# Three pairs of heads in flight in the sparse attention's loop, with the weights of the inner pairs normalised on GpSimd and both parts of the outputs made on VectorE

## The chip, the cores and the metric

One core of a Trainium2 chip runs the whole program. The metric is device time in microseconds (us), the median of three runs of one launch; lower is better.

## What is computed

Two blocks of a small transformer on 256 tokens of width 1024, in float32. The first block's first layer is a sparse attention: an indexer scores all keys for each query, the best 64 are kept, and the 16 heads (64 wide, two key and value heads) attend to those alone:

```python
topk = min(INDEX_TOPK, T // 4)
...
score = jnp.where(causal[None], score, -jnp.inf)
_, sel = lax.top_k(score, topk)
...
logits = jnp.where(valid[:, :, None, None, :], logits, -jnp.inf)
p = jax.nn.softmax(logits, axis=-1).astype(dt)
o = jnp.einsum('bqgrk,bqkgd->bqgrd', p, v_sel)
...
return out @ w_o
```

Behind it come a feed-forward layer, a gated linear recurrence with its own feed-forward layer, and then a second block (a gated linear attention beside a latent attention, and a feed-forward layer). They are not touched by the change.

## The kernel before

The program is written engine by engine, each with its own queue and explicit waits on semaphores; nothing reorders it. All weights come in tiles of 128x2048 through a ring of six staging buffers (`stage`). A product in float32 precision is made from two rounded parts of each operand: ScalarE rounds a tile to its upper part `wh` (`hi`, line 389), GpSimd subtracts it from the tile for the lower part `wl` (`lo`, line 393), and TensorE makes three products (lines 409 to 411). The activations have the two parts `xh` and `xl` in the same way. `low_ready` makes TensorE wait for the lower part of the tile that it is about to use; tile 8, the last of the output projection (`LAST_WO`), gets its lower part from VectorE (line 2598), all others from GpSimd.

The sparse attention's loop (`attend_pe`, `attend_act`, `attend_dve`) goes over eight pairs of heads. `sbias`, made from the selection, masks what a query doesn't attend to. For a pair i:

- TensorE makes the logits of both heads (`logits`, lines 808 and 810) in PSUM banks 0 and 1 or 2 and 3, by turns.
- VectorE scales and masks them and finds the negative of the largest of each row (`masked`, line 903) in a buffer `lg` in SBUF, of which there are three; the two query blocks have 128 and 256 keys, so each step has four instructions a pair, two of 128x128 and two of 128x256.
- ScalarE takes the exponentials with their sums (`exps`, line 874).
- VectorE takes the reciprocals of the sums (line 910) and scales the weights (`normalised`, line 916), a TENSOR_SCALAR in place in `lg`.
- TensorE transposes the weights (line 859) into banks 4 and 5, which all pairs share; ScalarE copies them to `pts` (line 883).
- TensorE multiplies them with the values (`value`, lines 820 to 824) into bank 6 or 7.
- ScalarE copies the result to `xh` (line 1021) and VectorE subtracts for `xl` (line 1136).

TensorE's queue holds logits 0 and 1, eleven fillers that keep it busy (`keep_warm`, line 687), and then for each i: logits i+2, transposes i, value i-1. ScalarE's holds exponentials 0, two copies of turned queries, exponentials 1, and then for each i: weight copy i, output copy i-1, exponentials i+2. VectorE's holds for each i: masking i+2, normalisation i+1, the lower part of output i-1. In the listings of the trace `arena` is the SBUF region in which `lg`, `pts`, the queries and the keys lie, and `ps` is PSUM.

GpSimd has no part in the loop: it makes the lower part of tile 6, waits for all eight normalisations, and then makes that of tile 7 (in the block at the end of `build`). Behind the loop TensorE makes the output projection with tiles 5 to 8 (`rows_t`), which waits for the last outputs' lower part, and ScalarE, which rounded the tiles up to 7 ahead of the loop, loads two rows of gains and goes on with tile 8.

Of the kernel before, what the change touches and what calls it, by code (L numbers as in the profile page):

```python
# [11 lines left out]
ALU = mybir.AluOpType  # L12
ACT = mybir.ActivationFunctionType
# [3 lines left out]
T = 256  # L17
D = 1024
P = 128
# [5 lines left out]
HEADS, HD, KVH = 16, 64, 2  # L25
# [150 lines left out]
def build(nc, A, out, marks):  # L176
    ctx = ExitStack()
    at = [SCRATCH + 128]
    with ctx:
# [89 lines left out]
        score = cut(12800, 3 * P)  # L269
        top8 = cut(13184, 2, 8)  # L270
        wi = cut(13200, 2, IH)
        lg = [cut(at, 2, 3 * P) for at in (13216, 13984, 12288)]
        pts = cut(14752, 2, 2, 3 * P)
        kit, kis = cut(16288, T), cut(16544, 2, P)
        relu0 = cut(14752, IH, P)
# [43 lines left out]
        def signals(names):  # L319
            return [Signal(sem(n)) for n in names.split()]  # L320
# [19 lines left out]
        lg_ps, nmx_ready, p_ready, pn_ready, pt_ps, pts_done, ot_ps, oh_done = signals(  # L340
            "lg_ps nmx_ready p_ready pn_ready pt_ps pts_done ot_ps oh_done")
        s_done, h_mul, h_ready = signals("s_done h_mul h_ready")


# [493 lines left out]
        def attend_pe(pe, pairs, logits, weighted, warm=0):  # L838
            def value(i):
                pe.wait_ge(pts_done.sem, pts_done.due(pe))  # L840
                if i >= 2:

                    pe.wait_ge(x_ready.sem, x_ready.due(pe))
                weighted(i, pts[:, i % 2, :, :]).then_inc(ot_ps.sem, ot_ps.up())

            for i in range(2):
                logits(i).then_inc(lg_ps.sem, lg_ps.up())
            keep_warm(4, warm)
            for i in range(pairs):
                if i + 2 < pairs:  # L850
                    pe.wait_ge(nmx_ready.sem, nmx_ready.due(pe))
                    logits(i + 2).then_inc(lg_ps.sem, lg_ps.up())
                pe.wait_ge(pn_ready.sem, pn_ready.due(pe))
                if i >= 1:

                    pe.wait_ge(pts_done.sem, pts_done.seen(pe) + 1)
                for e in range(2):
                    for c in range(3):
                        last = nc.tensor.transpose(ps[:, 4 + e, c * P:(c + 1) * P],
                                                   lg[i % 3][:, e, c * P:(c + 1) * P], ident[:])  # L860
# [6 lines left out]
        def attend_act(act, pairs, between, outputs):  # L867
            def exps(i):
                act.wait_ge(nmx_ready.sem, nmx_ready.due(act))
                for e in range(2):  # L870
                    for t, (c0, c1) in enumerate(((0, P), (P, 3 * P))):
                        at = 8 + 8 * (i % 2) + 2 * e + t
                        x = lg[i % 3][:, e, c0:c1]
                        ins = nc.scalar.activation(x, x, ACT.Exp, bias=small[:, at + 4:at + 5], scale=-1.0,  # L874
                                                   accum_out=small[:, 16 + at:17 + at])
                ins.then_inc(p_ready.sem, p_ready.up())

            exps(0)
            between()
            exps(1)  # L880
            for i in range(pairs):
                act.wait_ge(pt_ps.sem, pt_ps.due(act))
                nc.scalar.activation(pts[:, i % 2, :, :], ps[:, 4:6, 0:3 * P], ACT.Copy  # L883
                ).then_inc(pts_done.sem, pts_done.up())
                if i >= 1:
                    act.wait_ge(ot_ps.sem, ot_ps.due(act))
                    outputs(i - 1)
                if i + 2 < pairs:
                    exps(i + 2)
            act.wait_ge(ot_ps.sem, ot_ps.due(act))  # L890
            outputs(pairs - 1)

        def attend_dve(dve, pairs, scale, bias, outputs):
            def masked(i):
                dve.wait_ge(lg_ps.sem, lg_ps.due(dve))
                x = lg[i % 3]
                if i >= 3:

                    dve.wait_ge(pt_ps.sem, pt_ps.seen(dve) + i - 2)
                for e in range(2):  # L900
                    for t, (c0, c1) in enumerate(((0, P), (P, 3 * P))):
                        at = 12 + 8 * (i % 2) + 2 * e + t
                        ins = V.tensor_tensor_reduce(x[:, e, c0:c1], ps[:, 2 * (i % 2) + e, c0:c1], bias[:, c0:c1],
                                                     -scale, 3.0e38, ALU.add, ALU.min, small[:, at:at + 1])
                ins.then_inc(nmx_ready.sem, nmx_ready.up())

            def normalised(i):
                dve.wait_ge(p_ready.sem, p_ready.due(dve))
                at = 24 + 8 * (i % 2)
                V.reciprocal(small[:, at + 4:at + 8], small[:, at:at + 4]).then_inc(dve_step.sem, dve_step.up())  # L910
                dve.wait_ge(dve_step.sem, dve_step.now())
                for e in range(2):
                    for t, (c0, c1) in enumerate(((0, P), (P, 3 * P))):
                        x = lg[i % 3][:, e, c0:c1]
                        w = at + 4 + 2 * e + t
                        ins = V.tensor_scalar(x, x, small[:, w:w + 1], None, ALU.mult)
                ins.then_inc(pn_ready.sem, pn_ready.up())

            masked(0)
            masked(1)  # L920
            normalised(0)
            for i in range(pairs):
                if i + 2 < pairs:
                    masked(i + 2)
                if i + 1 < pairs:
                    normalised(i + 1)
                if i >= 1:
                    dve.wait_ge(oh_done.sem, oh_done.due(dve))
                    outputs(i - 1)
            pt_ps.skip(dve, pairs)  # L930
            dve.wait_ge(oh_done.sem, oh_done.due(dve))
            outputs(pairs - 1)

        def dsa_act(act):
# [82 lines left out]

            queries_turned((0, 1))

            def outputs(i):  # L1020
                nc.scalar.activation(xh[:, i, :], ps[:, 6 + i % 2, 0:T], ACT.Copy
                ).then_inc(oh_done.sem, oh_done.up())

            attend_act(act, HEADS // 2, lambda: queries_turned((2, 3)), outputs)

        def dsa_dve(dve):
            dve.wait_ge(cqh_done.sem, cqh_done.due(dve))
# [105 lines left out]
            dve.wait_ge(sel_done.sem, sel_done.now())  # L1133

            def outputs(i):
                V.tensor_tensor(xl[:, i, :], ps[:, 6 + i % 2, 0:T], xh[:, i, :].bitcast(F32), ALU.subtract  # L1136
                ).then_inc(x_ready.sem, x_ready.up())

            attend_dve(dve, HEADS // 2, HD ** -0.5, sbias[:], outputs)

        def head_sum_pool(pool):

# [1421 lines left out]
        @block.gpsimd  # L2564
        def _(pool):
            setup_pool(pool)
            for n in range(2, 6):
                lo(pool, n)
            dsa_pool(pool)

            def until(n, m):
                for i in range(n, m):
                    lo(pool, i)

            lo(pool, 6)
# [75 lines left out]
```

## Time and profile before

| | |
|---|---|
| median of 3 runs | 1050.39 us (1050.32 to 1051.92) |
| profiled execution: its time | 1050.05 us |
| its span | 1048.2 us |
| TensorE matmul busy | 1028.5 us, 98% |
| VectorE busy | 464.2 us, 44% |
| ScalarE busy | 560.6 us, 53% |
| GpSimd busy | 794.5 us, 76% |
| sparse attention's loop | from about 51 to 78.9 us of the span |
| mean granted TensorE clock | 0.999 |

The span is what the trace covers; the profiled execution's own time has 1.85 us around it. Times in the trace count from the start of the span. PE is TensorE's matrix multiply, PEld its weight loads, DVE VectorE, ACT ScalarE, POOL GpSimd, SP the queue of loads. A duration in a listing overlaps a little with that of the next instruction on the same engine, so the rounds below are measured from start to start.

### The profile page before, as it was taken

How to read it: one execution, taken by the hardware profiler on the slowest of the kernel's cores; microseconds unless marked ns; L12 is line 12 of the kernel's file. 1: busy time of each engine (PE TensorE's matmuls, PEld its weight loads, DVE VectorE, ACT ScalarE, POOL GpSimd, SP SyncE). 2: the span in 40 equal slices, each digit the busy share in tenths (PEclk: the TensorE clock that was granted, in tenths of full speed). 3: DMA queues.
4: the chain of work that ended last, by engine and by line, in shares of the span. 5: the costliest groups of instructions: out<-in, count | busy, mean ns of one | idle time of the engine just before them, and what ended most of it. 6: DMA issues, size and time to landing. Idle time of an engine off the chain costs nothing.

```text
span 1048.2 us, 17970 instructions
## 1 busy us (share of the span) xinstructions
PE 1028.5 (98%) x7744; PEld 951.0 (91%) x7744; DVE 464.2 (44%) x757; ACT 560.6 (53%) x779; POOL 794.5 (76%) x238
## 2 busy tenths in 40 slices
PE   7989999999999999999999999999999999999997
PEld 7868899998889997899998899999999988999986
DVE  4874263349825775317321142921253252533303
ACT  6684544443358775454444256466568356444420
POOL 4826898879678756889888779687674968988880
PEclk9999999999999999999999999999999999999999
DMA  9405555555545332765555356454443655555541
GB/s 361 155 2 182 219 201 188 188 191 198 198 169 196 123 121 85 250 249 195 184 189 195 134 194 235 164 198 144 178 162 116 207 197 187 197 202 189 184 151 40
DMA packets 27454, 186.59 MB, mean 178 GB/s; under 512 B 3168, under 2 KB 3424, under 8 KB 5872
## 3 DMA queue, kind: packets, MB, share of 16 engines
q1 hardware_dynamic: 25184, 178.83, 47.2%
q10 hardware_dynamic: 2192, 6.62, 2.0%
q8 instruction: 61, 1.00, 0.4%
q14 instruction: 17, 0.14, 0.0%
HBM read 184.39 MB, written 1.05 MB: 177 GB/s over the span
## 4 chain that ended last, share of the span: by engine, by line
PE 93%; ACT 2%; DVE 2%; POOL 1%; DMA 1%; issue 0%; DVEq 0%; SPq 0%; POOLq 0%
PE ps L409 29%; PE ps L411 29%; PE ps L410 28%; ACT arena L874 1%; PE ps L1528 1%; PE ps L1199 1%; DMA stage<-in_tiles 1%; PE ps L2242 1%; ACT arena L883 0%; POOL wl L393 0%; PE ps L760 0%; DVE arena L1087 0%; PE ps L2247 0%; PE ps L1546 0%; DVE arena L1082 0%
## 5 line engine op out<-in xcount | busy, mean ns | idle before, releaser
L393 POOL TENSOR_TENSOR wl<-stage,wh 128x2048 fp32r<-128x2048 f32 x165 | 762.6, 4644 | 209.3 <-ACT wh L389 189.0
L389 ACT ACTIVATE wh<-stage 128x2048 fp32r<-128x2048 f32 (+1 forms) x167 | 317.8, 1907 | 113.5 <-DMA stage<-in_tiles 112.7
L409 PE MATMUL ps<-xh,wh 128*128 128x256 f32 x1328 | 369.7, 278 | 1.4 <-DVE wl L536 1.4
L410 PE MATMUL ps<-xl,wh 128*128 128x256 f32 x1328 | 368.0, 277 | 0.0
L411 PE MATMUL ps<-xh,wl 128*128 128x256 f32 x1328 | 368.0, 277 | 0.0
L409 PEld LDWEIGHTS ps<-xh,wh 128*128 128x128 f32 x1328 | 249.7, 188 | 3.8 <-DVE wl L536 1.6
L410 PEld LDWEIGHTS ps<-xl,wh 128*128 128x128 f32 x1328 | 250.1, 188 | 0.1
L411 PEld LDWEIGHTS ps<-xh,wl 128*128 128x128 f32 x1328 | 249.3, 188 | 0.0
L409 PE MATMUL ps<-wh,xh 128*128 128x512 f32 (+2 forms) x400 | 134.4, 336 | 1.2 <-DVE xl L1136 0.9
L411 PE MATMUL ps<-wh,xl 128*128 128x512 f32 (+2 forms) x400 | 132.4, 331 | 0.0
L410 PE MATMUL ps<-wl,xh 128*128 128x512 f32 (+2 forms) x400 | 132.3, 331 | 0.0
L409 PE MATMUL ps<-wh,hh 128*128 128x512 f32 x312 | 121.9, 391 | 0.0
L410 PE MATMUL ps<-wl,hh 128*128 128x512 f32 x312 | 121.4, 389 | 0.0
L1452 DVE TENSOR_TENSOR hl<-arena,hh 128x256 fp32r<-128x256 f32 x54 | 107.9, 1999 | 9.0 <-ACT hh L1413 9.0
L411 PE MATMUL ps<-wh,hl 128*128 128x512 f32 x280 | 109.0, 389 | 0.0
L1430 ACT ACTIVATE arena<-ps 128x256 f32<-128x256 f32 x54 | 20.7, 384 | 150.8 <-PE ps L411 150.8
L1467 DVE TENSOR_TENSOR arena<-arena,ps 128x256 f32<-128x256 f32 x54 | 22.7, 421 | 167.8 <-ACT arena L1430 166.1
L409 PEld LDWEIGHTS ps<-wh,xh 128*128 128x128 f32 x400 | 75.2, 188 | 9.7 <-DVE xl L1136 1.2
L411 PEld LDWEIGHTS ps<-wh,xl 128*128 128x128 f32 x400 | 75.2, 188 | 7.7
L410 PEld LDWEIGHTS ps<-wl,xh 128*128 128x128 f32 x400 | 75.3, 188 | 7.1
L409 PEld LDWEIGHTS ps<-wh,hh 128*128 128x128 f32 x312 | 58.6, 188 | 11.8
L410 PEld LDWEIGHTS ps<-wl,hh 128*128 128x128 f32 x312 | 58.6, 188 | 11.8
(381 smaller groups left out, 1136.6 us busy)
## 6 DMA issues: line engine op xcount, KB each, us to landing
stage<-in_tiles SPq DMA_DIRECT2D x167, 1024.0 KB, 4.9
arena<-in_ln_g ACTq DMA_DIRECT2D x4, 512.0 KB, 3.8
arena<-in_ln_b ACTq DMA_DIRECT2D x4, 512.0 KB, 5.1
arena<-in_x_t SPq DMA_DIRECT2D x1, 1024.0 KB, 5.4
x_res<-in_x SPq DMA_DIRECT2D x1, 1024.0 KB, 21.0
out<-x_res SPq DMA_DIRECT2D x4, 256.0 KB, 2.0
stage<-in_tiles SPq DMA_DIRECT2D x1, 544.0 KB, 9.1
arena<-in_pre_mix_norm ACTq DMA_DIRECT2D x1, 512.0 KB, 6.8
```

The source lines that it names most:

```text
L389: nc.scalar.activation(tile_of(wh, n, *part), tile_of(stage, n, *part), ACT.Copy).then_inc(hi_done, 1)
L393: nc.gpsimd.tensor_tensor(tile_of(wl, n), tile_of(stage, n), tile_of(wh, n).bitcast(F32), ALU.subtract).then_inc(lo_done, 1)
L409: mm(out_, lh, rh, start=start, stop=False, skip_group_check=skip)
L410: mm(out_, lh, rl, start=False, stop=False, skip_group_check=skip)
L411: return mm(out_, ll, rh, start=False, stop=stop, skip_group_check=skip)
L874: ins = nc.scalar.activation(x, x, ACT.Exp, bias=small[:, at + 4:at + 5], scale=-1.0, accum_out=small[:, 16 + at:17 + at])
L1199: last = nc.tensor.transpose(ps[:, bank + b, k * P:(k + 1) * P], src[:, t, c:c + P], ident[:])
L1430: nc.scalar.activation(slot(silu_g, f), ps[:, G + f % 4, 0:T], ACT.Silu).then_inc(s_done.sem, s_done.up())
L1452: ins = V.tensor_tensor(hl[:, f, :], slot(hp, f), hh[:, f, :].bitcast(F32), ALU.subtract)
L1467: V.tensor_tensor(slot(hp, f), slot(silu_g, f), ps[:, G + f % 4, T:2 * T], ALU.mult).then_inc(h_mul.sem, h_mul.up())
L1528: mm(ps[c % 2 * CH:(c % 2 + 1) * CH, level_bank(h) + c // 2, column * CH:(column + 1) * CH], k_[:, t], q_[:, t], start=True, stop=True)
L2242: mm(ps[:, e, c0:c1], qn[:, 2 * i + e, y], kn[:, 2 * i + e, 0:c1 - c0], start=c0 == 0, stop=False, skip_group_check=True)
```

## The change

There are four weight buffers `lg` instead of three (the fourth at a free place of the arena), and the sums and maxima get a place for each of four pairs. TensorE makes the logits of pairs 0 to 2 ahead of the fillers and of pair i+3 in round i. ScalarE takes exponentials 2 and 3 behind weight copy 0 and exponentials i+3 behind copy i, and makes no output copies. VectorE masks i+3 in round i, takes all reciprocals, scales only pairs 0 and 7, and makes both parts of each output (copy, then subtraction). GpSimd scales pairs 1 to 6 (`normalised_pool`), two instructions a pair with the reciprocals spread over the keys; the wait for all eight normalisations ahead of tile 7 is gone. `shares_ready` counts reciprocals, `pn_ready` GpSimd's pairs, `ends_ready` VectorE's two.

```diff
-        lg = [cut(at, 2, 3 * P) for at in (13216, 13984, 12288)]
+        lg = [cut(at, 2, 3 * P) for at in (13216, 13984, 12288, 2048)]
...
-            for i in range(2):
+            for i in range(3):
+                if i == 2:
+                    pe.wait_ge(nmx_ready.sem, nmx_ready.due(pe))
                 logits(i).then_inc(lg_ps.sem, lg_ps.up())
             keep_warm(4, warm)
             for i in range(pairs):
-                if i + 2 < pairs:
+                if i + 3 < pairs:
                     pe.wait_ge(nmx_ready.sem, nmx_ready.due(pe))
-                    logits(i + 2).then_inc(lg_ps.sem, lg_ps.up())
-                pe.wait_ge(pn_ready.sem, pn_ready.due(pe))
+                    logits(i + 3).then_inc(lg_ps.sem, lg_ps.up())
+                if 0 < i < pairs - 1:
+                    pe.wait_ge(pn_ready.sem, pn_ready.due(pe))
+                else:
+                    pe.wait_ge(ends_ready.sem, ends_ready.due(pe))
...
                 nc.scalar.activation(pts[:, i % 2, :, :], ps[:, 4:6, 0:3 * P], ACT.Copy
                 ).then_inc(pts_done.sem, pts_done.up())
-                if i >= 1:
-                    act.wait_ge(ot_ps.sem, ot_ps.due(act))
-                    outputs(i - 1)
-                if i + 2 < pairs:
-                    exps(i + 2)
-            act.wait_ge(ot_ps.sem, ot_ps.due(act))
-            outputs(pairs - 1)
+                if i == 0:
+                    exps(2)
+                if i + 3 < pairs:
+                    exps(i + 3)
+            act.wait_ge(ot_ps.sem, pairs)
...
             def normalised(i):
                 dve.wait_ge(p_ready.sem, p_ready.due(dve))
-                at = 24 + 8 * (i % 2)
-                V.reciprocal(small[:, at + 4:at + 8], small[:, at:at + 4]).then_inc(dve_step.sem, dve_step.up())
-                dve.wait_ge(dve_step.sem, dve_step.now())
+                at = 44 + 12 * (i % 4)
+                V.reciprocal(small[:, at + 4:at + 8], small[:, at:at + 4]).then_inc(shares_ready.sem, shares_ready.up())
+                if 0 < i < pairs - 1:
+                    return
+                dve.wait_ge(shares_ready.sem, shares_ready.now())
...
-                ins.then_inc(pn_ready.sem, pn_ready.up())
-
-            masked(0)
-            masked(1)
-            normalised(0)
+                ins.then_inc(ends_ready.sem, ends_ready.up())
+
+            for i in range(3):
+                masked(i)
+            for i in range(2):
+                normalised(i)
             for i in range(pairs):
+                if i + 3 < pairs:
+                    masked(i + 3)
                 if i + 2 < pairs:
-                    masked(i + 2)
-                if i + 1 < pairs:
-                    normalised(i + 1)
+                    normalised(i + 2)
                 if i >= 1:
-                    dve.wait_ge(oh_done.sem, oh_done.due(dve))
+                    dve.wait_ge(ot_ps.sem, ot_ps.due(dve))
                     outputs(i - 1)
...
             def outputs(i):
+                V.tensor_copy(xh[:, i, :], ps[:, 6 + i % 2, 0:T]).then_inc(oh_done.sem, oh_done.up())
+                dve.wait_ge(oh_done.sem, oh_done.now())
                 V.tensor_tensor(xl[:, i, :], ps[:, 6 + i % 2, 0:T], xh[:, i, :].bitcast(F32), ALU.subtract
                 ).then_inc(x_ready.sem, x_ready.up())
...
+        def normalised_pool(pool, pairs):
+
+            for i in range(1, pairs - 1):
+                pool.wait_ge(shares_ready.sem, i + 1)
+                at = 48 + 12 * (i % 4)
+                for t, (c0, c1) in enumerate(((0, P), (P, 3 * P))):
+                    x = lg[i % 4][:, :, c0:c1]
+                    share = small[:, at + t:at + t + 3:2].unsqueeze(2).to_broadcast([P, 2, c1 - c0])
+                    ins = nc.gpsimd.tensor_tensor(x, x, share, ALU.mult)
+                ins.then_inc(pn_ready.sem, pn_ready.up())
...
             lo(pool, 6)
-            pool.wait_ge(pn_ready.sem, HEADS // 2)
+            normalised_pool(pool, HEADS // 2)
             lo(pool, 7)
```

TensorE's queue at the loop's start, before: two pairs of logits (808 and 810), the fillers (687), the logits of pair 2, the transposes of pair 0 (859), the logits of pair 3.

```order
L808 MATMUL ps<-arena 128x128 x2
L810 MATMUL ps<-arena 128x256 x2
L687 MATMUL ps<-ident 128x128 x11
L808 MATMUL ps<-arena 128x128 x2
L810 MATMUL ps<-arena 128x256 x2
L859 MATMUL ps<-ident,arena 128x128 x6
```

The same place after, from the logits of pair 1 on; the transposes are line 864 now.

```order
L808 MATMUL ps<-arena 128x128 x2
L810 MATMUL ps<-arena 128x256 x2
L808 MATMUL ps<-arena 128x128 x2
L810 MATMUL ps<-arena 128x256 x2
L687 MATMUL ps<-ident 128x128 x11
L808 MATMUL ps<-arena 128x128 x2
L810 MATMUL ps<-arena 128x256 x2
L864 MATMUL ps<-ident,arena 128x128 x6
```

The logits of pair 2 moved ahead of the fillers, and those of pair 3 ahead of the transposes of pair 0.

GpSimd's queue, the difference around the loop: line 654 is the last step of the queries' rotation, 393 a tile's lower part (the first is tile 6, the next tile 7), 1153 the scaling of one pair in two instructions, of which the middle pairs are left out here.

```order
 L654 TENSOR_TENSOR arena<-arena 128x8x8
-L393 TENSOR_TENSOR wl<-stage,wh 128x2048 x14
+L393 TENSOR_TENSOR wl<-stage,wh 128x2048
+L1153 TENSOR_TENSOR arena<-arena,small 128x2x128
+L1153 TENSOR_TENSOR arena<-arena,small 128x2x256
...
+L393 TENSOR_TENSOR wl<-stage,wh 128x2048 x13
```

Six pairs, twelve instructions, now stand between tile 6 and tile 7, and tile 7 follows the last of them in the queue.

ScalarE's queue at the loop's end, before: exponentials (874), weight copies (883), output copies (1021), the loads of gains, the tiles behind the loop (389).

```order
L874 ACTIVATE arena,small<-arena,small 128x256
L883 ACTIVATE arena<-ps 128x768
L1021 ACTIVATE xh<-ps 128x256
L883 ACTIVATE arena<-ps 128x768
L1021 ACTIVATE xh<-ps 128x256 x2
L1191 DMA arena<-in_ln_g 128x1024
L1191 DMA arena<-in_ln_b 128x1024
L389 ACTIVATE wh<-stage 128x2048 x3
```

After, where the exponentials are line 879 and the weight copies line 888:

```order
L879 ACTIVATE arena,small<-arena,small 128x256
L888 ACTIVATE arena<-ps 128x768 x3
L1206 DMA arena<-in_ln_g 128x1024
L1206 DMA arena<-in_ln_b 128x1024
L389 ACTIVATE wh<-stage 128x2048 x3
```

Behind the last exponentials there are three weight copies instead of two, and no output copy.

## Rows read from the trace of the kernel before

**Rows 1.** the waits of TensorE: who waited for whom: us in total, times, longest

```profile
PE ps L859 <- DVE arena L916: 3.4, 6, 1.0
```

**Rows 2.** timeline of ScalarE, one round: start, us, engine, line, operation, out<-in, count

```profile
63.98 0.39 ACT L874 ACTIVATE arena<-arena,small 128x128 f32<-128x128 f32 x1
...
65.74 0.79 ACT L883 ACTIVATE arena<-ps 128x768 f32<-128x768 f32 x1
66.43 0.37 ACT L1021 ACTIVATE xh<-ps 128x256 fp32r<-128x256 f32 x1
66.69 0.40 ACT L874 ACTIVATE arena<-arena,small 128x128 f32<-128x128 f32 x1
```

**Rows 3.** timeline of VectorE, one round

```profile
64.63 0.28 DVE L903 CUSTOM_DVE_ANT_0 arena<-ps,sbias 128x128 f32<-128x128 f32 x1
...
66.09 1.01 DVE L916 TENSOR_SCALAR arena<-arena,small 128x128 f32<-128x128 f32 x4
67.01 0.42 DVE L1136 TENSOR_TENSOR xl<-ps,xh 128x256 fp32r<-128x256 f32 x1
67.34 0.28 DVE L903 CUSTOM_DVE_ANT_0 arena<-ps,sbias 128x128 f32<-128x128 f32 x1
```

**Rows 4.** timeline of TensorE, then of ScalarE, at the loop's start

```profile
53.26 2.72 PE L687 MATMUL ps<-ident 128*128 128x128 f32 x22
55.91 0.49 PE L808 MATMUL ps<-arena 64*128 64x128 f32 x4
...
56.76 0.87 PE L859 MATMUL ps<-ident,arena 128*128 128x128 f32 x6
...
57.75 0.79 ACT L883 ACTIVATE arena<-ps 128x768 f32<-128x768 f32 x1
```

**Rows 5.** timelines of VectorE, ScalarE, GpSimd and TensorE at the loop's end

```profile
74.02 0.18 DVE L910 RECIPROCAL small<-small 128x4 f32<-128x4 f32 x1 [1.16 <-ACT arena L874]
74.23 1.01 DVE L916 TENSOR_SCALAR arena<-arena,small 128x128 f32<-128x128 f32 x4
...
78.40 0.43 DVE L1136 TENSOR_TENSOR xl<-ps,xh 128x256 fp32r<-128x256 f32 x1 [0.55 <-ACT xh L1021]
...
77.99 0.38 ACT L1021 ACTIVATE xh<-ps 128x256 fp32r<-128x256 f32 x1 [0.59 <-PE ps L824]
...
75.31 4.55 POOL L393 TENSOR_TENSOR wl<-stage,wh 128x2048 fp32r<-128x2048 f32 x1 [19.79 <-DVE arena L916]
...
75.29 0.87 PE L859 MATMUL ps<-ident,arena 128*128 128x128 f32 x6 [1.03 <-DVE arena L916]
...
78.89 0.50 PE L409 MATMUL ps<-wh,xh 128*128 128x512 f32 x1 [0.94 <-DVE xl L1136]
```

**Rows 6.** VectorE's groups by form: count, busy us, mean ns, idle before

```profile
L903 DVE CUSTOM_DVE_ANT_0 arena<-ps,sbias 128x256 f32<-128x256 f32 x16 | 6.7, 419 | 0.0
L916 DVE TENSOR_SCALAR arena<-arena,small 128x256 f32<-128x256 f32 x16 | 5.6, 347 | 0.0
...
L1071 DVE COPY arena<-ps 128x256 f32<-128x256 f32 x1 | 0.4, 425 | 1.3 <-PE ps L753 1.3
```

**Rows 7.** GpSimd's instructions on the arena: ns min/median/max, first and last start

```profile
L1151 POOL TENSOR_TENSOR arena<-arena x3: 463/742/1292, 39.9 to 42.0; 128x512 f32<-128x512 f32 x1, 128x256 f32<-128x256 f32 x1, 128x128 f32<-128x128 f32 x1
...
L1147 POOL TENSOR_TENSOR arena<-arena x2: 1040/1041/1042, 37.7 to 38.7; 128x512 f32<-128x512 f32 x2
```

**Rows 8.** timeline of GpSimd and VectorE, from 254; one line's durations

```profile
254.04 13.76 POOL L393 TENSOR_TENSOR wl<-stage,wh 128x2048 fp32r<-128x2048 f32 x3 [0.66 <-ACT wh L389]
...
258.76 4.52 DVE L585 TENSOR_SCALAR lmask<-arena 128x64 bf16<-128x64 f32 x1
...
L591 DVE TENSOR_SCALAR arena<-arena x6: 184/187/4593, 268.2 to 268.7; 128x64 f32<-128x64 f32 x6
```

**Rows 9.** TensorE's last instruction; a stretch's busy us by engine, granted clock

```profile
1042.09 0.39 PE L411 MATMUL ps<-wh,hl 128*128 128x512 f32 x1
...
1045.50:1046.00 0.50, 0.00 (x0) 0.00 (x0) 0.29 (x1) 0.00 (x0) 0.00 (x0) 0.96 0.01 4
```

More of the change, by code:

```diff
@@ L339, in build @@
         relu_sb, scored0 = signals("relu_sb scored0")
-        lg_ps, nmx_ready, p_ready, pn_ready, pt_ps, pts_done, ot_ps, oh_done = signals(
-            "lg_ps nmx_ready p_ready pn_ready pt_ps pts_done ot_ps oh_done")
+        lg_ps, nmx_ready, p_ready, shares_ready, pn_ready, ends_ready, pt_ps, pts_done, ot_ps, oh_done = signals(
+            "lg_ps nmx_ready p_ready shares_ready pn_ready ends_ready pt_ps pts_done ot_ps oh_done")
         s_done, h_mul, h_ready = signals("s_done h_mul h_ready")
@@ L859, in attend_pe @@
                         last = nc.tensor.transpose(ps[:, 4 + e, c * P:(c + 1) * P],
-                                                   lg[i % 3][:, e, c * P:(c + 1) * P], ident[:])
+                                                   lg[i % 4][:, e, c * P:(c + 1) * P], ident[:])
                 last.then_inc(pt_ps.sem, pt_ps.up())
@@ L865, in attend_pe, with attend_act @@
             nmx_ready.skip(pe, 2)
-        def attend_act(act, pairs, between, outputs):
+        def attend_act(act, pairs, between):
             def exps(i):
@@ L871, in exps @@
                     for t, (c0, c1) in enumerate(((0, P), (P, 3 * P))):
[L872 to L875, printed above, removed]
+                        at = 40 + 12 * (i % 4) + 2 * e + t
+                        x = lg[i % 4][:, e, c0:c1]
+                        ins = nc.scalar.activation(x, x, ACT.Exp, bias=small[:, at:at + 1], scale=-1.0,
+                                                   accum_out=small[:, 4 + at:5 + at])
                 ins.then_inc(p_ready.sem, p_ready.up())
@@ L895, in masked @@
                 dve.wait_ge(lg_ps.sem, lg_ps.due(dve))
-                x = lg[i % 3]
-                if i >= 3:
-                    dve.wait_ge(pt_ps.sem, pt_ps.seen(dve) + i - 2)
+                x = lg[i % 4]
+                if i >= 4:
+                    dve.wait_ge(pt_ps.sem, pt_ps.seen(dve) + i - 3)
                 for e in range(2):
                     for t, (c0, c1) in enumerate(((0, P), (P, 3 * P))):
-                        at = 12 + 8 * (i % 2) + 2 * e + t
+                        at = 40 + 12 * (i % 4) + 2 * e + t
                         ins = V.tensor_tensor_reduce(x[:, e, c0:c1], ps[:, 2 * (i % 2) + e, c0:c1], bias[:, c0:c1],
@@ L908, in normalised @@
                 dve.wait_ge(p_ready.sem, p_ready.due(dve))
-                at = 24 + 8 * (i % 2)
-                V.reciprocal(small[:, at + 4:at + 8], small[:, at:at + 4]).then_inc(dve_step.sem, dve_step.up())
-                dve.wait_ge(dve_step.sem, dve_step.now())
+                at = 44 + 12 * (i % 4)
[3 more added lines that the diff above has]
+                dve.wait_ge(shares_ready.sem, shares_ready.now())
                 for e in range(2):
                     for t, (c0, c1) in enumerate(((0, P), (P, 3 * P))):
-                        x = lg[i % 3][:, e, c0:c1]
+                        x = lg[i % 4][:, e, c0:c1]
                         w = at + 4 + 2 * e + t
                         ins = V.tensor_scalar(x, x, small[:, w:w + 1], None, ALU.mult)
-                ins.then_inc(pn_ready.sem, pn_ready.up())
-            masked(0)
-            masked(1)
-            normalised(0)
+                ins.then_inc(ends_ready.sem, ends_ready.up())
[3 more added lines that the diff above has]
+                normalised(i)
             for i in range(pairs):
+                if i + 3 < pairs:
+                    masked(i + 3)
                 if i + 2 < pairs:
-                    masked(i + 2)
-                if i + 1 < pairs:
-                    normalised(i + 1)
+                    normalised(i + 2)
                 if i >= 1:
-                    dve.wait_ge(oh_done.sem, oh_done.due(dve))
+                    dve.wait_ge(ot_ps.sem, ot_ps.due(dve))
                     outputs(i - 1)
             pt_ps.skip(dve, pairs)
-            dve.wait_ge(oh_done.sem, oh_done.due(dve))
+            dve.wait_ge(ot_ps.sem, ot_ps.due(dve))
             outputs(pairs - 1)
@@ L1018, in dsa_act @@
             queries_turned((0, 1))
[L1020 to L1024, printed above, removed]
+            attend_act(act, HEADS // 2, lambda: queries_turned((2, 3)))
         def dsa_dve(dve):
```

## Prediction

> **What bounds the kernel now.** I read the page first: TensorE is busy in 98% of the span, so away from the attention loop the time is TensorE's and the change touches nothing there; what the edit is worth is how much earlier or later TensorE starts the output projection behind the loop. Its table of waits says where TensorE loses time in the loop: six waits for VectorE's scaling of the weights, 3.4 us in all [rows 1]. Then the timeline, engine by engine. ScalarE's round for one pair is 2.71 us with no gap: four exponentials 1.76 (63.98 to 65.74), the copy of the turned weights 0.69, the upper part of the outputs 0.26 [rows 2]. VectorE's round is as long and as full: masking and the reciprocals 1.46, scaling 0.92, lower part 0.33 [rows 3]. TensorE needs less: a round whose transposes wait for nothing takes 2.46 us, and 0.2 or more is its wait for the scaling. So the inner rounds are bound by ScalarE and VectorE together, the first by the order of TensorE's queue, and the last two by a chain that passes from engine to engine [rows 4, 5].
>
> **The start.** Three logits now stand ahead of TensorE's eleven fillers instead of two. The third waits for pair 0's maxima, which are there when the fillers began before, 53.26. One pair's logits take 0.85 (55.91 to 56.76) and the fillers 2.65 (53.26 to 55.91) [rows 4]. So transposes 0, behind third logits, fillers and fourth logits, start at 53.26 + 0.85 + 2.65 + 0.85 = 57.61 rather than 56.76, and take 0.87. ScalarE was free for its copy at 57.75 [rows 4] and now waits to about 58.55: **+0.80**. VectorE masks pair 2 meanwhile and scales pair 0 by about 57.0, under the fillers.
>
> **The rounds.** ScalarE loses the 0.26, so its round is 1.76 + 0.69 = 2.45. VectorE loses the scaling and gains a copy: a 128x256 copy out of PSUM takes 0.425 [rows 6]; with the subtraction behind it, about 0.79 from first to next. 1.46 + 0.79 = 2.25, below ScalarE. TensorE's 2.46 is just level. GpSimd scales a pair in two instructions, 2x128 and 2x256 elements per partition. Nearest rows: its products with a spread operand take 1.04 for 512 elements; its sums of two full operands take 0.46, 0.74 and 1.29 for 128, 256 and 512 [rows 7]. I take 1.04 + 0.66 (the 0.46 raised by the slope to 1.04) = 1.70, the spread operand being the nearest form; below stands 1.04 + 0.46 = 1.50, above 0.74 + 1.29 = 2.03. All are under 2.45, and a pair has two rounds of slack between its exponentials and its transposes, so in the rounds this is hidden. The Trainium skill (GPSIMD Engine Reference, 3.1 Elementwise) gives about 2.6 cycles an element for any two-input operation, spread or not; by its measured 4497 ns for 2048 elements this would be an estimate of 1.7 to 1.8 here, and the end would move by 0.1 at most.
>
> ScalarE's order puts the exponentials of pair 7 behind copy 4, no longer behind copy 5. Before, reciprocals 7 start at 74.02, released by the last exponential [rows 5]. Five output copies (1.30) and one weight copy (0.69) no longer stand before it, and the start adds 0.80: 72.83. Pair 6's exponentials are 2.45 earlier: reciprocals 6 at 70.38.
>
> **The end.** This is where I think it is lost. GpSimd had waited for all eight scalings before it made the low part of tile 7, which started at 75.31 and takes 4.5 us [rows 5]. Now it starts that straight behind pair 6: 70.38 + 0.21 (reciprocals to next, 74.02 to 74.23) + 0.07 (VectorE's last scaling, 74.23 + 1.01, to GpSimd's 75.31) + 1.70 = 72.36, and reads SBUF until 72.36 + 4.55 = 76.91. Pair 7 is still scaled by VectorE, which is ready for it at 72.83 + 0.21 = 73.04. The trace shows what happens to a VectorE instruction of this kind under such a GpSimd instruction: a TENSOR_SCALAR of 128x64 from SBUF to SBUF takes 0.19 by the median and 4.59 at the most; another starts at 258.76, lasts 4.52 and ends at 263.28, as does the second of three tiles' low parts of 4.6 that began at 254.04 [rows 8]. That the loop's own TENSOR_SCALAR is of the kind that is held follows from its speed: 128x256 in 0.347 against 0.425 for the copy out of PSUM [rows 6]. Masking, which reads PSUM and one tensor of SBUF, is not held: its 16 large instructions take 0.419 in the mean [rows 6], though the first ones ran beside tile 6's low part; nor is the output step, of the same kind. The Trainium skill (SBUF, Who interferes with whom) speaks against the change in the same way: a VectorE operation that takes both SBUF ports and a GpSimd operation exclude each other for a whole instruction, whoever is first. By that rule, the trace agrees, with 4.59 us for an instruction whose median is 0.19.
>
> So the first of the four scalings ends 0.1 behind 76.91 and the rest 0.75 later: 77.76. From there the old chain runs: before, from the end of the scaling (75.24) through transposes, weight copy, values and outputs to TensorE's restart at 78.89 is 3.65 [rows 5]; VectorE's copy instead of ScalarE's adds 0.05 (before, 77.99 to 78.40 for the same step). Restart at 77.76 + 3.70 = 81.46, **2.6 us later**. Tile 7's low part is needed only by the third tile of the projection, later than it is ready in either kernel; tile 8's, on VectorE, moves with ScalarE's tiles, which follow the loop. What comes after is TensorE's queue and shifts whole.
>
> Sum against the profiled execution: 1050.05 + 2.6 = 1052.65. It lies 0.34 under the median of the runs, so for a median 1050.39 + 2.6 = **1053.0**. With 1.50 and 2.03 for GpSimd's pair, the shift is 2.4 or 2.9.
>
> **Rivals.**
> *No hold, no gain: 1050.4.* If VectorE is not held, it scales pair 7 from 73.04 to 74.05. But transposes 6 wait for copy 5 (it ends at 72.7 + 0.8 = 73.5), copy 6 ends at 75.25, transposes 7 start at 75.3, against 75.29 before [rows 5]. Two rounds then stand in a chain of copy, transposes, copy, and the gained 1.2 us of ScalarE are spent waiting: shift about 0. This is the not-slower side. It decides if tile 7's low part starts only after 74.0, or if this TENSOR_SCALAR isn't of the held kind. Against: 72.36 is 1.7 under 74.0, and rows 6 and 8 show the kind. Chance 0.15, with 0.02 of it below the 0.2% bound.
> *More than one hold, or a slow GpSimd: about 1054.5.* The stepped, spread share could cost GpSimd twice my price: pair 6 ends 1.7 later and all behind it too, 1053.0 + 1.7 = 1054.7. Nothing in the trace reads a step of two. Chance 0.08.
> *The clock falls: 1054.5 to 1056.* Between values 5 (about 75.1) and transposes 7 (77.8) TensorE would stand for 2.7 us. At the program's end, after the last matmul (1042.09 + 0.39), the half microsecond from 1045.5 was granted 0.96 in the mean [rows 9]: a clock that falls from 1.00 to 0.50, the 1.2 GHz level, gives this by falling at 1045.96, when TensorE had done nothing for 3.5 us. As long a stretch at half speed would cost half of itself, 1.7 us: 1054.7. The Trainium skill (TensorE: Matmul & The Clock Gate, Part 1) has an idle TensorE fall to 1.2 GHz; no row has a gap of 2.7 us inside the work. Chance 0.05.
> *The change gains its rounds: 1048.* If some other order shortened the chain at the end, at most the 2.0 us taken off ScalarE would come back. Nothing speaks for it. Chance 0.02.
>
> **Numbers.** The forecast itself has 0.70. A measurement of this kernel can tell 0.2%, 2.1 us, from no change. The forecast's own range, 1052.1 to 1053.7 (2.4 to 2.9, and 0.4 for shifts of phase later), lies a little over the bound of 1052.5: a fifth or more of it counts as the same. Slower: 0.70 x 0.7 + 0.13 = 0.62; same: 0.70 x 0.3 + 0.13 = 0.34; faster: 0.04. The range takes in the case without a hold and the dearer ones: 1050.1 to 1054.8.
>
> **What would show it.** In the profile after: ScalarE's first weight copy at 58.5; rounds of 2.45; GpSimd's pairs at 1.7; its next tile at about 72.4; the first TENSOR_SCALAR of pair 7 lasting some 4 us and ending with that tile; TensorE's projection at 81.5. Wrong, if that TENSOR_SCALAR takes 0.3, if the tile starts after 74, or if TensorE's clock is below 1.00 near 80.

## The result and the profile after

The changed kernel takes 1053.86 us in the median of 8 runs (1052.96 to 1055.86) against 1050.49 us of the kernel before (8 runs): the ratio is 1.0028, with a 95% interval of 1.0019 to 1.0037. It is slower by 3.4 us. The profiled execution has a span of 1051.6 us; the one before had 1048.2.

Both executions reach the loop with some tenths' difference from the work ahead of it, which the change doesn't touch, so I measure the loop from TensorE's first logits to its first projection matmul. Before, this is 50.96 to 78.89, 27.93 us. After:

```profile
51.39 0.49 PE L808 MATMUL ps<-arena 64*128 64x128 f32 x4 [0.33 <-DVE sbias L1122]
...
75.20 0.39 PE L824 MATMUL ps<-arena 128*64 128x128 f32 x4
77.89 1.54 PE L864 MATMUL ps<-ident,arena 128*128 128x128 f32 x6 [2.30 <-DVE arena L921]
79.36 0.70 PE L820 MATMUL ps<-arena 128*64 128x128 f32 x4
...
82.81 0.50 PE L409 MATMUL ps<-wh,xh 128*128 128x512 f32 x1 [0.99 <-DVE xl L1140]
```

This is TensorE's timeline of the changed kernel (start, us, line, operation, what ended the idle time before it). From 51.39 to 82.81 there are 31.42 us: 3.49 more, as much as the whole loss (this loop begins 0.43 us later, and what follows it is 0.5 us shorter). Before, transposes 7 waited 1.03 us for VectorE's scaling and were in place at 75.29 [rows 5]. Here they wait 2.30 us and begin at 77.89, and take 1.54 us instead of 0.87. Two things went wrong, one behind the other. The first is in GpSimd's and VectorE's timelines at the loop's end:

```profile
70.94 1.61 POOL L1153 TENSOR_TENSOR arena<-arena,small 128x256 f32<-128x256 f32 x2 [0.83 <-DVE small L913]
72.51 4.52 POOL L393 TENSOR_TENSOR wl<-stage,wh 128x2048 fp32r<-128x2048 f32 x1
```

```profile
73.13 0.18 DVE L913 RECIPROCAL small<-small 128x4 f32<-128x4 f32 x1 [1.47 <-ACT arena L879]
73.34 4.49 DVE L921 TENSOR_SCALAR arena<-arena,small 128x128 f32<-128x128 f32 x4
77.75 0.41 DVE L1138 CAST xh<-ps 128x256 fp32r<-128x256 f32 x1
```

GpSimd scales pair 6 in 1.61 us and starts tile 7's low part at 72.51; it ends at 77.03. VectorE's four TENSOR_SCALARs of pair 7, 1.01 us before [rows 5], start at 73.34 and last 4.49 us; they end at 77.83. Of the line's eight instructions the shortest takes 274 ns, the median 340 and the longest 3767: a single one is held, and it ends 0.1 us behind the tile.

```profile
L921 DVE TENSOR_SCALAR arena<-arena,small x8: 274/340/3767, 56.2 to 77.5; 128x128 f32<-128x128 f32 x4, 128x256 f32<-128x256 f32 x4
```

The second is the clock. These are stretches of the changed kernel, with the busy time of each engine and then the granted clock:

```profile
77.50:78.00 0.50, 0.11 (x1) 0.12 (x2) 0.50 (x3) 0.00 (x0) 0.00 (x0) 0.90 0.00 0
78.00:79.00 1.00, 1.00 (x5) 1.00 (x6) 0.93 (x4) 0.00 (x0) 0.00 (x0) 0.50 0.00 0
81.25:81.50 0.25, 0.25 (x8) 0.25 (x6) 0.22 (x2) 0.00 (x0) 0.00 (x0) 0.87 0.00 0
```

TensorE, granted 1.00 until then, goes to 0.50, the 1.2 GHz level, at about 77.9 (a mean of 0.90 in the half microsecond from 77.5) and is back at about 81.3. Before that it had done nothing from 75.59 to 77.89. The last transposes and values run in this stretch.

The rest of the loop went as the change says. ScalarE's rounds are 2.44 us instead of 2.71 [rows 2], with one wait of 0.72 at the start:

```profile
59.00 0.81 ACT L888 ACTIVATE arena<-ps 128x768 f32<-128x768 f32 x1 [0.72 <-PE ps L864]
...
63.22 0.79 ACT L888 ACTIVATE arena<-ps 128x768 f32<-128x768 f32 x1
...
65.66 0.80 ACT L888 ACTIVATE arena<-ps 128x768 f32<-128x768 f32 x1
...
74.82 0.81 ACT L888 ACTIVATE arena<-ps 128x768 f32<-128x768 f32 x1 [1.03 <-PE ps L864]
79.47 0.81 ACT L888 ACTIVATE arena<-ps 128x768 f32<-128x768 f32 x1 [3.83 <-PE ps L864]
```

### The profile page after: what moved, and what is told of

It is laid out like the page before. It is cut to its first block, busy times and chain, and to the rows that moved or that the text cites. A ratio compares the mean times of both kernels' runs of the same rounds, so it can differ in the third digit from the quotient of the medians.

```text
span 1051.6 us, 17956 instructions
## 1 busy us (share of the span) xinstructions
PE 1030.3 (98%) x7744; PEld 953.0 (91%) x7744; DVE 462.2 (44%) x741; ACT 558.0 (53%) x771; POOL 803.5 (76%) x250
## 4 chain that ended last, share of the span: by engine, by line
PE 93%; DVE 2%; ACT 2%; POOL 1%; DMA 1%; issue 0%; DVEq 0%; SPq 0%; POOLq 0%
PE ps L409 29%; PE ps L411 28%; PE ps L410 28%; PE ps L1543 1%; ACT arena L879 1%; PE ps L1214 1%; DMA stage<-in_tiles 1%; PE ps L2257 0%; POOL wl L393 0%; DVE arena L921 0%; PE ps L760 0%; ACT arena L888 0%; DVE arena L1089 0%; PE ps L2262 0%; PE ps L1561 0%; DVE arena L1084 0%
## 5 line engine op out<-in xcount | busy, mean ns | idle before, releaser
L1467 DVE TENSOR_TENSOR hl<-arena,hh 128x256 fp32r<-128x256 f32 x54 | 104.9, 1943 | 9.0 <-ACT hh L1428 9.0
```

Of the source, the lines that this page charges most:

```text
L1467: ins = V.tensor_tensor(hl[:, f, :], slot(hp, f), hh[:, f, :].bitcast(F32), ALU.subtract)
```

## The experiments

I held three theories against each other: that the early tile 7 holds VectorE's scaling and the pause lets the clock fall (mine); that the loss lies in the rounds, the start or GpSimd's price; that the early tile costs by itself. In the diffs lines of "..." are left out code.

**The wait put back (e1_guard).**

```diff
             normalised_pool(pool, HEADS // 2)
+            pool.wait_ge(ends_ready.sem, 2)
             lo(pool, 7)
```

> The changed kernel, and GpSimd waits for both of VectorE's scalings (pairs 0 and 7) before it makes the low part of tile 7. My theory (the low part of tile 7 holds VectorE's scaling of pair 7, and the pause lets TensorE's clock fall): the four TENSOR_SCALARs take 1.0 us together instead of 4.5, transposes 7 start right after weight copy 6 (some 2.2 us earlier than in the changed kernel), the granted clock stays 1.00, and the time is that of the kernel before, 1050.5 +- 0.4: the whole 3.4 us go, and nothing of ScalarE's shorter rounds is left, because the last two rounds are a chain of copy, transposes, copy. Rival (the loss lies in the rounds, in the later start or in GpSimd's share of the scaling): 1052.5 or more stays. Second rival (the hold had hidden a gain of the rounds): 1049 or less.

Measured: 1050.42 us, the kernel before 1050.45 beside it, ratio 1.0007 (0.9998 to 1.0015). From first logits (50.91) to projection 28.00 us. Timelines of VectorE, then GpSimd, then TensorE:

```profile
72.86 1.01 DVE L921 TENSOR_SCALAR arena<-arena,small 128x128 f32<-128x128 f32 x4
```

```profile
73.95 4.54 POOL L393 TENSOR_TENSOR wl<-stage,wh 128x2048 fp32r<-128x2048 f32 x1 [1.88 <-DVE arena L921]
```

```profile
75.30 0.84 PE L864 MATMUL ps<-ident,arena 128*128 128x128 f32 x6 [0.19 <-ACT arena L888]
...
78.91 0.50 PE L409 MATMUL ps<-wh,xh 128*128 128x512 f32 x1 [0.98 <-DVE xl L1140]
```

The scaling takes 1.01 us again, transposes 7 wait for ScalarE's copy 6 and not for VectorE, and the projection starts 28.00 us after the first logits, against 27.93 in the kernel before. One wait takes away the 3.4 us; what is left of the change is worth nothing that these runs can tell from zero. Both rivals fall.

**Pair 7 on GpSimd as well (e2_pool7).**

```diff
-            for i in range(1, pairs - 1):
+            for i in range(1, pairs):
                 pool.wait_ge(shares_ready.sem, i + 1)
...
-                if 0 < i < pairs - 1:
+                if i > 0:
                     return
```

TensorE waits for GpSimd's count for all pairs but 0 in it.

> The changed kernel, and pair 7 is scaled by GpSimd as well; tile 7 follows it with no wait, so nothing that VectorE does in the loop's end can be held. My theory: GpSimd's pair 7 takes 1.6 us from its reciprocals against VectorE's 1.0, both end before weight copy 6 does, so the time is that of the run with the wait, 1050.5 +- 0.4, although tile 7 starts early here too. Rival (it is the early tile itself that costs, through ports or the tile's buffer): 1052.5 or more.

Measured: 1050.66 us, ratio 1.0006 (0.9998 to 1.0015), and again 28.00 us from first logits to projection. Tile 7 starts at 74.86 there, under VectorE's output steps, and those take their usual 0.42:

```profile
73.29 1.61 POOL L1153 TENSOR_TENSOR arena<-arena,small 128x256 f32<-128x256 f32 x2 [0.83 <-DVE small L913]
74.86 4.54 POOL L393 TENSOR_TENSOR wl<-stage,wh 128x2048 fp32r<-128x2048 f32 x1
```

```profile
75.54 0.42 DVE L1138 CAST xh<-ps 128x256 fp32r<-128x256 f32 x1 [1.56 <-PE ps L824]
76.00 0.42 DVE L1140 TENSOR_TENSOR xl<-ps,xh 128x256 fp32r<-128x256 f32 x1
```

Copies out of PSUM and subtractions with one operand in PSUM are not held here. That an early tile costs nothing by itself this run shows only in part, since its tile 7 starts 23.57 us after the first logits, later than with the wait (23.04), against 21.12 in the changed kernel. The changed kernel's own trace says the rest: under its early tile, transposes 6 take 0.84 us and weight copy 6 takes 0.81 (0.85 and 0.81 in e1_guard, whose tile starts 0.5 us behind the start of its transposes 6), and only the TENSOR_SCALAR is longer.

**The hold alone, in the kernel before (e3_before_early_tile).**

```diff
             lo(pool, 6)
-            pool.wait_ge(pn_ready.sem, HEADS // 2)
+            pool.wait_ge(pn_ready.sem, HEADS // 2 - 1)
             lo(pool, 7)
```

> The kernel before, in which GpSimd waits for seven normalisations instead of eight before tile 7: the hold alone, without any of the change. My theory: tile 7's low part runs from about 72.6 to 77.1 and VectorE's scaling of pair 7, due at 74.2, ends at about 78.0 instead of 75.2: 2.7 us later, 1053.2; if TensorE's clock falls in the pause of 3.7 us as it did in the changed kernel, about 1 us more, 1054.3. Rival (the hold needs something else of the change): 1050.5.

Measured: 1057.02 us, ratio 1.0060 (1.0047 to 1.0074): more than twice what I expected of the hold. Timelines and stretches of its profile:

```profile
74.47 4.51 POOL L393 TENSOR_TENSOR wl<-stage,wh 128x2048 fp32r<-128x2048 f32 x1 [17.11 <-DVE arena L916]
```

```profile
76.10 3.69 DVE L916 TENSOR_SCALAR arena<-arena,small 128x128 f32<-128x128 f32 x4
```

```profile
52.83 0.49 PE L808 MATMUL ps<-arena 64*128 64x128 f32 x4 [0.39 <-DVE sbias L1120]
...
79.85 1.54 PE L859 MATMUL ps<-ident,arena 128*128 128x128 f32 x6 [3.72 <-DVE arena L916]
...
85.09 0.79 PE L409 MATMUL ps<-wh,xh 128*128 128x512 f32 x1 [0.94 <-DVE xl L1136]
85.68 0.63 PE L410 MATMUL ps<-wl,xh 128*128 128x512 f32 x1
86.10 0.63 PE L411 MATMUL ps<-wh,xl 128*128 128x512 f32 x1
```

```profile
79.00:85.00 6.00, 4.30 (x30) 3.57 (x30) 1.94 (x7) 1.58 (x3) 0.00 (x0) 0.50 0.00 0
89.00:90.00 1.00, 1.00 (x5) 0.77 (x4) 0.31 (x1) 1.00 (x1) 1.00 (x1) 0.89 0.00 0
```

The hold is there (3.69 us instead of 1.01) with no other part of the change, and it is as long as I said. The clock's share was not: in a pause of 3.72 us it falls, at about 79.0, and it stays at 0.50 for some 10 us, to about 89.1 (a mean of 0.89 from 89 to 90), so that the projection's first matmuls run on it too (0.42 us from one to the next, 85.68 to 86.10, against 0.23 in the kernel before). The loop takes 32.26 us, 4.33 more than before. The profiled execution took 1058.16 us, 8.1 more than that of the kernel before; 1.9 of them lie ahead of the loop, which begins at 52.83 instead of 50.96, after another fall of the clock at about 10.7 that the edit has no part in (see the last section). The six runs reach from 1053.73 us, at a mean granted clock of 0.998, to 1058.74 at 0.993, so the median is no price of the hold alone.

**The clock apart from the hold (e4_fillers).**

```diff
+                if i == pairs - 1:
+                    keep_warm(0, 9)
                 if 0 < i < pairs - 1:
                     pe.wait_ge(pn_ready.sem, pn_ready.due(pe))
```

> The changed kernel, with nine filler matmuls (2.2 us) on TensorE before it waits for pair 7's scaling, into a bank that is free by then. It separates the clock from the hold. My theory: the hold stays (the TENSOR_SCALARs take 4.5 us), the granted clock stays 1.00 through 78 to 82, and the projection starts 1.2 us earlier against the end of the scaling: 3.7 us after it, not 5.0; time 1052.6. Rival (the tail from the scaling to the projection is long for another reason, and the clock's fall costs nothing): 1053.9.

Measured: 1053.64 us in the median (11 runs, 1051.96 to 1055.05), ratio 1.0027 (1.0019 to 1.0036). The profile does what was expected: clock 1.00, the hold in place (4.49 us), 30.13 us from first logits to projection, and its execution took 1052.0. The median doesn't: it lies where the changed kernel's does. The runs fall in two groups, four from 1051.96 to 1052.33 (and one at 1053.07) and six from 1053.64 to 1055.05. That left it open, so I ran it once more, with the changed kernel on the same chip. A fall of the clock ahead of the loop, as in e3_before_early_tile, would part the runs in this way; no profile of the slower group was kept, so this is not shown.

**The same pair on one chip (e8_changed_again and e9_fillers_again).** No edit in the first; the second is e4_fillers.

> The changed kernel once more, unedited, as the partner on the same chip for the next run. My theory: 1053.5 to 1054, with the granted clock at 0.50 for some us around 79 in its profile. Rival (the spread of its runs, 1053.0 to 1055.9, is not the clock): a profile in which the clock stays 1.00 and the time is the same.

> The changed kernel with nine fillers ahead of the wait for pair 7's scaling, as in the earlier run whose two halves lay 2 us apart (five runs near 1052.2, six near 1054.1). My theory, by the earlier profile (from the end of the scaling to the projection 3.7 us, not 5.0): 1.2 us under the changed kernel of the same call. Rival (the clock's fall costs nothing in the median): no difference.

Measured: 1054.43 us (ratio 1.0028, 1.0019 to 1.0038) and 1052.81 us (ratio 1.0013, 1.0004 to 1.0022), with the kernel before at 1051.56 beside them: 1.6 us between the two, where I expected 1.2. The two intervals overlap, and the first pair of medians (1053.86 and 1053.64) lay only 0.2 apart, so the clock's price rests on the profiles. The changed kernel's profiled execution did not do what I expected, and told me more that way. It was the fastest of its ten, 1051.83 us, and its clock stayed at 1.00:

```profile
72.96 4.48 DVE L921 TENSOR_SCALAR arena<-arena,small 128x128 f32<-128x128 f32 x4
```

```profile
51.00 0.49 PE L808 MATMUL ps<-arena 64*128 64x128 f32 x4 [0.34 <-DVE sbias L1122]
...
81.13 0.50 PE L409 MATMUL ps<-wh,xh 128*128 128x512 f32 x1 [0.98 <-DVE xl L1140]
```

```profile
77.00:79.00 2.00, 1.49 (x18) 1.29 (x18) 1.93 (x6) 0.59 (x1) 0.00 (x0) 1.00 0.00 0
```

Same program, same hold, same 2.29 us without work on TensorE, but no fall: 30.13 us, as in both filler runs (30.13 and 30.14). So the hold alone is worth 2.20 us (30.13 less 27.93), the fall 1.29 (31.42 less 30.13), and the fall happens in some executions and not in others: in two of three profiles with the pause, and in neither of the two with fillers in it. The mean granted clock of each run over its whole span orders the ten runs the same way: the one at 1.000 took 1051.83 us, the four at 0.998 to 0.999 took 1053.4 to 1053.7, and the five at 0.995 to 0.997 took 1055.2 to 1056.8. A mean over the span doesn't say where the clock was lower, and the kernel before has most of its runs at 0.998 and 0.999 too, so this doesn't count how often it fell in the loop.

**The end of the chain (e6_banks).** With the wait of e1_guard.

```diff
+        def turned_bank(i, pairs):
+            return 2 * (i % 2) if i >= pairs - 2 else 4
...
-                if i >= 1:
+                if 1 <= i < pairs - 2:
                     pe.wait_ge(pts_done.sem, pts_done.seen(pe) + 1)
+                bank = turned_bank(i, pairs)
```

> The changed kernel with the wait ahead of tile 7 (as in the first run), and the transposes of pairs 6 and 7 go to PSUM banks 0 and 1, and 2 and 3, which the logits have left by then, instead of 4 and 5; so they don't wait for the weight copy of the pair before. My theory (the last two rounds are a chain of copy, transposes, copy through the one pair of banks, which eats ScalarE's gain): weight copies 5 and 6 follow each other at 0.7 to 1.0 us, not 1.84, and the projection starts 1.0 us earlier than with the wait alone: 1049.4. Rival (ScalarE's shorter rounds are spent elsewhere): 1050.4.

Measured: 1050.87 us, the kernel before 1051.56, ratio 0.9992 (0.9983 to 1.0002): a gain that the interval doesn't quite clear. The trace is clear. ScalarE's timeline, last three weight copies:

```profile
72.92 0.80 ACT L892 ACTIVATE arena<-ps 128x768 f32<-128x768 f32 x1
73.91 0.81 ACT L892 ACTIVATE arena<-ps 128x768 f32<-128x768 f32 x1 [0.19 <-PE ps L867]
75.52 0.81 ACT L892 ACTIVATE arena<-ps 128x768 f32<-128x768 f32 x1 [0.80 <-PE ps L867]
```

Copies 5 and 6 are 0.99 us apart, against 1.84 in the changed kernel (72.98 to 74.82), and 26.94 us pass from first logits (51.31) to projection (78.25): 1.06 less than with the wait alone.

**Fewer fillers besides (e7_both) and alone (e5_start).** Six instead of eleven; e7_both on e6_banks, e5_start on e1_guard.

```diff
-            attend_pe(pe, HEADS // 2, logits, weighted, 11)
+            attend_pe(pe, HEADS // 2, logits, weighted, 6)
```

> As the run before, and six fillers instead of eleven at the loop's start. My theory: the first weight copy, which waited 0.7 to 0.8 us for transposes 0 behind logits and fillers, comes 0.6 us earlier (VectorE's scaling of pair 0 ends then), everything behind it too: 1048.8, under both kernels. Rivals: the clock falls at the loop's start with fewer fillers (a stretch of 0.50 there, 1050 or more); or the start is hidden by the end (1049.4, no gain over the run before).

> The changed kernel with the wait ahead of tile 7, and six fillers instead of eleven, the banks as they were. My theory: the first weight copy comes 0.7 us earlier and the chain at the end starts from it, so 0.7 to 0.8 us less from the first logits to the projection: 27.2 instead of 28.0, the median 0.7 under the kernel before. Rival (the end hides the start): no change, 28.0.

Measured for e7_both: 1049.29 us, the kernel before 1051.56 beside it, ratio 0.9981 (0.9972 to 0.9989). It is the one kernel here that beats the kernel before clear of its interval, and it lies 5.1 us under the changed kernel measured beside it (1054.43).

```profile
51.06 0.49 PE L808 MATMUL ps<-arena 64*128 64x128 f32 x4 [0.37 <-DVE sbias L1126]
...
56.98 0.88 PE L867 MATMUL ps<-ident,arena 128*128 128x128 f32 x6 [0.18 <-DVE arena L925]
...
77.22 0.50 PE L409 MATMUL ps<-wh,xh 128*128 128x512 f32 x1 [0.98 <-DVE xl L1144]
```

```profile
57.89 0.81 ACT L892 ACTIVATE arena<-ps 128x768 f32<-128x768 f32 x1
```

26.16 us; ScalarE doesn't wait for its first copy. e5_start: 1050.13 us, before 1050.39, ratio 0.9994 (0.9985 to 1.0003), and 27.21 us from first logits (52.91) to projection (80.12), 0.79 less than with the wait alone, as expected; the median shows 0.3 of it, which can't be told from nothing. The two savings add up: 28.00 less 0.79 less 1.06 is 26.15.

**The banks in the kernel before (e10_before_banks).** The edit of e6_banks there.

> The kernel before, with the transposes of pairs 6 and 7 in the banks that the logits have left. In it transposes 6 and 7 wait for VectorE's scaling and not for the weight copy before them, so my theory says no change (within 0.2 us of the kernel before), though the same edit took 1.0 us off the changed kernel with the wait. Rival (the banks are worth something by themselves): 0.5 us or more under the kernel before.

Measured: 1050.68 us, the kernel before 1050.39, ratio 1.0001 (0.9992 to 1.0010), 27.94 us from first logits to projection: nothing. Where the scaling is the last to come, the banks are free in time anyway.

**One part of the change alone (e11_upper_only).**

```diff
-                if i >= 1:
-                    act.wait_ge(ot_ps.sem, ot_ps.due(act))
-                    outputs(i - 1)
                 if i + 2 < pairs:
                     exps(i + 2)
...
             def outputs(i):
+                V.tensor_copy(xh[:, i, :], ps[:, 6 + i % 2, 0:T]).then_inc(oh_done.sem, oh_done.up())
+                dve.wait_ge(oh_done.sem, oh_done.now())
```

> The kernel before, with only the outputs' upper part moved from ScalarE to VectorE: one part of the change alone. My theory (VectorE's round is as full as ScalarE's before the change, so this part needs GpSimd's scaling beside it): VectorE's round grows from 2.71 to about 3.15 us, ScalarE waits in each, and the time is 2.5 us over the kernel before. Rival (ScalarE alone bounds the rounds): rounds of 2.45 and 1 to 2 us under it.

Measured: 1050.59 us, ratio 0.9999 (0.9990 to 1.0008). I was wrong about the sum, though not about the round. ScalarE's weight copies:

```profile
58.23 0.79 ACT L883 ACTIVATE arena<-ps 128x768 f32<-128x768 f32 x1
...
60.67 0.79 ACT L883 ACTIVATE arena<-ps 128x768 f32<-128x768 f32 x1
...
63.12 0.81 ACT L883 ACTIVATE arena<-ps 128x768 f32<-128x768 f32 x1
...
66.02 0.81 ACT L883 ACTIVATE arena<-ps 128x768 f32<-128x768 f32 x1 [0.20 <-PE ps L859]
...
69.05 0.81 ACT L883 ACTIVATE arena<-ps 128x768 f32<-128x768 f32 x1 [0.20 <-PE ps L859]
...
75.12 0.81 ACT L883 ACTIVATE arena<-ps 128x768 f32<-128x768 f32 x1 [0.20 <-PE ps L859]
77.14 0.81 ACT L883 ACTIVATE arena<-ps 128x768 f32<-128x768 f32 x1 [1.20 <-PE ps L859]
```

The middle rounds, three from 66.02 to 75.12, are 3.03, and their transposes wait for VectorE. But the first two are 2.44 and 2.45, while VectorE still has its lead, the third is 2.90, and the last is 2.02, since VectorE has nothing left to mask. In the kernel before the same seven are 2.44, 2.84, four near 2.71 and 2.34. So three rounds lose 0.3 each and the third 0.2, while the second and the last gain 0.4 and 0.3: the loop is 0.50 longer (28.43 from first logits to projection), not 2.5. I had multiplied one round's excess by the rounds, which holds only in the middle of a loop of eight.

## Why the prediction was right, and where it was off

The forecast was 2.6 us slower by the hold, 1053.0 us; measured were 3.4 us, 1053.86. That is inside the full range (1050.1 to 1054.8) and 0.2 above the narrow one of the forecast itself (1052.1 to 1053.7). By its steps (times of the changed kernel less the 0.43 by which its loop began later):

- The start: transposes 0 at 57.66 against 57.61, copy 0 at 58.57 against 58.55; +0.80 was right.
- The rounds: 2.44 against 2.45. GpSimd's pair took 1.61, not 1.70: I had raised the shorter instruction to 0.66 and it takes 0.61. The estimate of 1.7 to 1.8 beside it, which took a spread operand to cost as much as a full one, is further off.

```profile
L1153 POOL TENSOR_TENSOR arena<-arena,small x12: 612/826/1041, 58.6 to 71.5; 128x256 f32<-128x256 f32 x6, 128x512 f32<-128x512 f32 x6
```

- The end: reciprocals 7 at 72.70 against 72.83, tile 7 at 72.08 against 72.36, end of the scaling at 77.40 against 77.76. That a TENSOR_SCALAR is held to the end of GpSimd's tile was read from rows 8, and it came out: the first of the four lasts 3.77 us and ends 0.1 behind the tile. The shift of the projection without the clock is 2.20 us in three executions, against 2.6: the reciprocals and GpSimd's pair were 0.13 too late and 0.13 too long, and smaller terms made the rest.
- From the scaling's end to the projection: 3.70 forecast, 3.69 in the executions that kept their clock (e8_changed_again: 77.44 to 81.13), 4.98 in the first profile. This is the term that was mis-sized. The fall of the clock stood among the rivals, with a chance of 0.05 and a price of 1.7 us on top of the hold. It came true in the profile, where its price is 1.29. That it did so in most runs is likely, since the median's 3.4 us less the hold's 2.20 leave 1.2, but it isn't shown. The sum had put the fall at nothing, and a clock below 1.00 near 80 was one of my own signs of being wrong; it was 0.50 there. I had read rows 9 as comfort: TensorE did nothing for 3.5 us there before the clock fell, and my pause was to be 2.7. Here it fell at the end of a pause of 2.30. The Trainium skill (TensorE: Matmul & The Clock Gate, Part 1) has an idle TensorE fall to 1.2 GHz, and I should have given this rule more weight than one row.
- The rival without a hold said no gain: 1050.4 with the shift at zero. The run with the wait put back is that case, 28.00 us against 27.93, and e6_banks shows its reason, the chain through one pair of banks.

So the sign, the mechanism and the place were right, and the size was short by the clock. Two errors of opposite sign met: 0.4 too much for the hold, and 1.2 to 1.3 left out for the clock. That the total came as near as 0.9 us is in part luck.

What stays open: what decides whether the clock falls after such a pause. Up to the pause I found no difference that would explain it between the two traces of the changed kernel: from 51 to 77 us TensorE is busy for 20.92 us in the one and 20.86 in the other, at a clock of 1.00 in both.

## What to carry to other kernels

A wait that looks idle can be a guard: before you take one away, ask what the released instruction holds. In these runs a TENSOR_SCALAR between SBUF buffers that begins under GpSimd's long subtraction waits for all that is left of it: a 4.5 us tile started 0.8 us before a 1 us scaling made that scaling end 3.5 us late, and 2.20 of this reached TensorE. When an edit shortens the rounds of a short loop, look for what its first and last rounds wait on; here the start and the end of the loop took back what the shorter rounds gave, and two small edits there (free banks, fewer fillers) brought 1.85 us. And a new pause on TensorE can cost more than its length: one of 2.3 us brought 1.29 us more in one execution and nothing more in another.

## What the runs showed of the hardware

- The clock can fall after 2.30 us without matmuls and, in the same program, stay after 2.29. Once down, it was back after 3.4 us in one profile and after 10 us in e3_before_early_tile, where TensorE was busy for 4.30 of the 6 us from 79 to 85.
- It can fall after a shorter pause, and while TensorE is at work again. Near the program's start, far ahead of the loop, TensorE ends a row of fillers at 9.06 in the profile of e5_start and starts its first product at 10.84; the clock goes to 0.50 at about 11.6 and is back at about 15.0. Its row and three stretches:

```profile
10.84 0.38 PE L409 MATMUL ps<-xh,wh 128*128 128x256 f32 x1 [1.77 <-DVE wl L536]
11.00:12.00 1.00, 1.00 (x8) 1.00 (x9) 1.00 (x3) 1.00 (x3) 0.00 (x0) 0.80 1.01 426
12.00:13.00 1.00, 1.00 (x7) 1.00 (x6) 0.94 (x2) 0.62 (x1) 0.00 (x0) 0.50 1.07 451
15.00:16.00 1.00, 1.00 (x11) 1.00 (x10) 0.86 (x5) 0.40 (x1) 0.52 (x1) 0.99 1.03 434
```

- The same place has a pause of 2.28 us and a fall in e3_before_early_tile, and the other eleven profiles have pauses of 0.88 to 1.42 us and no fall there. With the fall the loops start at 52.91 and 52.83 instead of about 51, so it costs some 1.8 us that has nothing to do with the edits. Part of the spread of a few microseconds between executions of one kernel is likely this, but only these profiles show it.
- Under GpSimd's tile VectorE's reciprocals, its masking from PSUM, its copy out of PSUM (a CAST here) and its subtraction with one operand in PSUM keep their usual times (0.18 us; 0.29 and 0.42 under tile 6; 0.42; 0.42); only the TENSOR_SCALAR between SBUF buffers is held.
